# Two-block transformer on one core: first down projection of the second feed-forward accumulates onto a residual that ScalarE puts into PSUM

## Chip, cores and metric

The kernel runs on one core of one Trainium2 chip. The metric is the device time of one execution in microseconds. Before the change the median of three runs is 1496.56 us (1496.21 to 1496.62).

## What is computed

Two transformer blocks over 512 tokens of width 1024, in f32. The first has a mixed attention stage and a gated feed-forward; the second has two kinds of attention, a cross-attention, and at its end the feed-forward that matters here:

```python
def second_block(x, ...):
        ...
        h = rms_norm(x, norm_mlp[l])
        x = x + jnp.square(jax.nn.relu(h @ w_up[l])) @ w_down[l]
    return rms_norm(x, norm_final)
```

`w_up` is 1024 x 4096 and `w_down` 4096 x 1024.

## The kernel before

All activations lie transposed, features on the partitions: `x` is 8 chunks of 128 features x 512 tokens. Every f32 operand of a large product is split into a high part and a rest (`wh`, `wl` for weights, `hh`, `hl` or `ah2`, `al2` for activations), and a product is three matmuls of 128x128 by 128x512 (`three`, L1166 to L1170). Weights come as a stream of panels, 512 KB each, which hold 8 tiles of 128x128; a panel is 24 matmuls. The ring has four slots: SyncE loads a panel into `stage`, ScalarE copies it to `wh` (`hi`, L521 to L528), VectorE writes the rest `wl` (`lo`, L754 to L764). `hi` of a panel waits until TensorE is done with the panel four earlier, since it overwrites its `wh`.

The order on each engine is written out by hand, with semaphores between them. The second feed-forward runs as two halves of 2048 hidden features, A and B:

- Up: four rounds of four panels (`up_body`, one for each engine). TensorE makes a unit of 128 hidden features in one of PSUM's banks 0 to 3. VectorE scales it out of PSUM into `tmp` (L769), makes the rest of the weight panel four ahead (L764), squares it behind a relu (L2111), ScalarE copies the high part into `ah2` (L516), VectorE makes the rest `al2` (L2102).
- Down: eight chunks of 128 output features, each of two panels, so 48 matmuls over the 16 hidden units (`down_loop`). The first matmul of a chunk overwrites its bank, the others accumulate. At the end of a chunk VectorE adds the bank to `x` (L2125) and counts `evac`. ScalarE has nothing to do there but the weight copies.

TensorE goes from the last up panel of half A straight on to the first down panel. Of each chunk of the down projection `begin` (L1172 to L1176) waits for the panel's `wl` and for the eviction of the bank's last user, four units before:

```python
    def begin(p, e):
        pe.wait_ge(s.lo_ready, p.index + 1)
        if e is not None:
            pe.wait_ge(s.evac, e - 3)
```

ScalarE's last round of half A is `up_body(P_UP_A, FH // 4 - 1, False, 0)`, followed by `down_loop(P_DOWN_A, E_DOWN_A, False)`. In it, `hi` at `u == 3` prepares the fourth down panel and waits for the last up panel to be done. Half B has the same shape; its down projection (`last` is true) is tied to the final norm and is not changed.

Of the kernel before, what the change touches and what calls it, by code (L numbers as in the profile page):

```python
# [25 lines left out]
ALU = mybir.AluOpType  # L26
ACT = mybir.ActivationFunctionType
AX_X = mybir.AxisListType.X
# [3 lines left out]
KT = D // P  # L32
T = 512
# [25 lines left out]
FH = FF2 // P // 2  # L59
# [83 lines left out]
def semaphores(nc):  # L143

    s = Names()

    def named(names):
        return [nc.alloc_semaphore(name) for name in names.split()]
# [10 lines left out]
        "sums col_done mean_ready pow_done")  # L159
    (s.rs_ready, s.row_done, s.row_ready, s.u_ready) = named(  # L160
        "rs_ready row_done row_ready u_ready")
    (s.va_gelu, s.ln_mean, s.ln_pow, s.v_normed) = named(
        "va_gelu ln_mean ln_pow v_normed")
    (s.ws_masked, s.spatial_done, s.pooled, s.poolmm_done) = named(
        "ws_masked spatial_done pooled poolmm_done")
    (s.lam_dots, s.lam_exps, s.v_done, s.qk_hi) = named(
        "lam_dots lam_exps v_done qk_hi")
    (s.qk_ready, s.v_hi, s.v_ready, s.bias_in) = named(
        "qk_ready v_hi v_ready bias_in")
    (s.score_done, s.scored, s.negated, s.exped) = named(  # L170
# [338 lines left out]
def scalar_program(nc, act, s, b, dram, scratch, line_dram, out):  # L509
    A = nc.scalar.activation  # L510
# [75 lines left out]
    act.wait_ge(s.line_copied, 1)  # L586
    act.dma_start(line_dram, b.lines[0:HEADS, :]).then_inc(s.lines_out, 16)
    hi(Panel(P_POOL + 1 + RING))
    act.wait_ge(s.lam_dots, 1)
    A(b.lam_e, b.lam_d, ACT.Exp).then_inc(s.lam_exps, 1)  # L590

    act.wait_ge(s.lines_out, 16)
# [122 lines left out]
    for i in range(2):  # L715
        for c in range(4):
            k = 4 * i + c
# [29 lines left out]
def vector_program(nc, dve, s, b):  # L747
    V = nc.vector
# [66 lines left out]
    lam = b.early[:, 768:1024].rearrange("p (a c d) -> p a c d", a=2, c=2)  # L815
    prod = b.tmp[:, 0, 0:128].rearrange("p (a d) -> p a d", a=2)
    st.link(V.tensor_tensor(prod, lam[:, :, 0, :], lam[:, :, 1, :], ALU.mult))
    V.tensor_reduce(b.lam_d, prod, AX_X, ALU.add).then_inc(s.lam_dots, 1)
    dve.wait_ge(s.consts_in, 16)


# [10 lines left out]
    for t in range(TT):  # L832
        ins = V.tensor_scalar(b.va[:, t, :], b.ps[:, 2 + t // 2, 256 * (t % 2):256 * (t % 2) + 256],
                              b.rs[:, t:t + 1], None, ALU.mult)
# [8 lines left out]
        st.link(V.bn_stats(b.ln_stats[:, 6 * t:6 * t + 6], b.va[:, t, :]))  # L843
        st.link(V.bn_aggr(b.ln_mv[:, 2 * t:2 * t + 2], b.ln_stats[:, 6 * t:6 * t + 6]))
    var = b.ln_mv.rearrange("p (t c) -> p t c", c=2)
    V.tensor_scalar(b.ln_var, var[:, :, 1], 1e-5, None, ALU.add).then_inc(s.ln_mean, 1)
    evac_row(Panel(P_POOL + 1), E_POOL + 1, b.xb[:, 1, 16:], 1)
    lo(Panel(P_POOL + 1 + RING))
    dve.wait_ge(s.ln_pow, 1)
# [36 lines left out]
    with dve.Fori(0, 2) as i:  # L886
        for u in range(RING):
            e = E_Q + u
# [121 lines left out]
    for i in range(2):  # L1010
        for u in range(4):
            j = 4 * i + u
            p = Panel(P_PROJ + u + RING * i)
# [104 lines left out]
def gpsimd_program(nc, pool, s, b):  # L1118
    G = nc.gpsimd
    G.memset(b.lines[0:HEADS, T:LINE], NEG).then_inc(s.lines_set, 1)  # L1120

    pool.wait_ge(s.early_in, 64)
    G.affine_select(out=b.ws[:], in_=b.ws[:], compare_op=ALU.is_ge, fill=0.0, base=0,
                    pattern=[[0, 4], [1, P]], channel_multiplier=-1).then_inc(s.ws_masked, 1)

    def power(n):
        pool.wait_ge(s.mean_ready, n)
        G.tensor_tensor(b.rs, b.mean, b.expo[:, 0:4], ALU.pow).then_inc(s.pow_done, 1)

    power(1)  # L1130
    pool.wait_ge(s.ln_mean, 1)
    G.tensor_tensor(b.ln_rs, b.ln_var, b.expo[:, 0:4], ALU.pow).then_inc(s.ln_pow, 1)
    pool.wait_ge(s.omean_ready, 1)
    G.tensor_tensor(b.ors, b.omean, b.expo, ALU.pow).then_inc(s.opow_done, 1)
    power(2)

    pool.wait_ge(s.mean_ready, 3)
    G.tensor_tensor(b.rsa, b.mean, b.expo[:, 0:4], ALU.pow).then_inc(s.pow_a, 1)
    pool.wait_ge(s.mean_b, 1)
    G.tensor_tensor(b.rs, b.mean, b.expo[:, 0:4], ALU.pow).then_inc(s.pow_done, 1)  # L1140
    pool.wait_ge(s.mmean_ready, 1)
    G.tensor_tensor(b.mrs, b.mmean, b.expo[:, 0:MT], ALU.pow).then_inc(s.mpow_done, 1)
    pool.wait_ge(s.pv_done, 12)
    pool.wait_ge(s.v_ready, 8)
    pool.wait_ge(s.turned_ready, 48)
    G.memset(b.a[:], 0.0).then_inc(s.a_cleared, 1)
    pool.wait_ge(s.panel_done, P_VG + 4)
    G.memset(b.ke[:], 0.0).then_inc(s.ke_cleared, 1)

    for n in range(2):  # L1150
        pool.wait_ge(s.gmean_ready, n + 1)
        G.tensor_tensor(b.grs[:, 8 * n:8 * n + 8], b.gmean[:, 8 * n:8 * n + 8], b.expo[:, 0:8],
                        ALU.pow).then_inc(s.gpow_done, 1)
    for n in (4, 5):
        power(n)
    for half in range(2):
        pool.wait_ge(s.mean_ready, 6 + half)
        pair = slice(2 * half, 2 * half + 2)
        G.tensor_tensor(b.rs[:, pair], b.mean[:, pair], b.expo[:, 0:2], ALU.pow).then_inc(s.pow_done, 1)
# [3 lines left out]
def tensor_program(nc, pe, s, b):  # L1163
    MM = nc.tensor.matmul

    def three(out, wh, wl, xh, xl, start, stop):  # L1166

        MM(out, wh, xh, start=start, stop=False, skip_group_check=True)  # L1168
        MM(out, wh, xl, start=False, stop=False, skip_group_check=True)  # L1169
        return MM(out, wl, xh, start=False, stop=stop, skip_group_check=True)  # L1170
# [8 lines left out]
        wh, wl = parts_of(b, p)  # L1179
        return wh[:, a:a + n], wl[:, a:a + n]  # L1180

    def features(p, e, slot, xh=None, xl=None, tiles=range(KT), last=KT, width=T, ready=None, between=None):


        xh, xl = (b.hh, b.hl) if xh is None else (xh, xl)
        begin(p, e)
        for n, k in enumerate(tiles):
            for step in (between or {}).get(n, ()):
                step()
            if ready:  # L1190
                ready(k)
            wh, wl = w(p, P * n)
            ins = three(b.ps[:, slot, 0:width], wh, wl, xh[:, k, 0:width], xl[:, k, 0:width], k == 0, k == last - 1)
        ins.then_inc(s.panel_done, 1)

    def column_sums(n, sums):
# [269 lines left out]
def block2_scalar(nc, act, s, b, dram, scratch, A, AR, hi, row, x_parts, x_square, residual_loop, exp_pair):  # L1466
# [207 lines left out]
    residual_loop(P_XO, E_XO, "norm_mlp", 4)  # L1674


    def up_body(p0, i, first, base):
        for u in range(4):
            hi(Panel(p0 + u + RING, RING, i))
            if first and u == 0:  # L1680
                row(5)
            act.wait_ge(s.acted2, base + 4 * i + u + 1)
            AR(b.ah2[:, 4 * i + u, :], b.tmp[:, u % 2, :], ACT.Copy).then_inc(s.act2_hi, 1)

    def down_loop(p0, e0, last):
        if last:
            act.wait_ge(s.sums, 46)
        def body(i):
            for c in range(4):
                k = 4 * i + c  # L1690
                for m in range(2):
                    hi(Panel(p0 + 2 * c + m + RING, 8, i))
                if last and k == KT - 1:
                    act.wait_ge(s.sums, 45 + k)
                    for half in range(2):
                        act.wait_ge(s.evac, e0 + k + 1 + half)
                        tok = slice(M * half, M * half + M)
                        A(b.tmp[:, 1, tok], b.x[:, k, tok], ACT.Square).then_inc(s.x_squared, 1)
                elif last:
                    act.wait_ge(s.sums, 45 + k)  # L1700
                    act.wait_ge(s.evac, e0 + k + 1)
                    x_square(k, c % 2)
                    AR(b.x[:, k, :], b.x[:, k, :], ACT.Copy, scale=col(b, "norm_final", k)).then_inc(s.x_second, 1)

        body(0)
        body(1)

    up_body(P_UP_A, 0, True, 0)
    with act.Fori(1, FH // 4 - 1) as i:
        up_body(P_UP_A, i, False, 0)  # L1710
    up_body(P_UP_A, FH // 4 - 1, False, 0)
    down_loop(P_DOWN_A, E_DOWN_A, False)
    with act.Fori(0, FH // 4 - 1) as i:
        up_body(P_UP_B, i, False, FH)
# [5 lines left out]
def block2_vector(nc, dve, s, b, st, lo, evac_row, mean, x_rest, x_sum, residual_loop, score_pair):  # L1720
# [394 lines left out]
    def down_loop(p0, e0, last):  # L2115
        def body(i):
            for c in range(4):
                k = 4 * i + c
                if last and k == KT - 1:
                    continue  # L2120
                for m in range(2):
                    p = Panel(p0 + 2 * c + m, 8, i)
                    dve.wait_ge(s.panel_done, p.index + 1)
                    if m == 1:
                        V.tensor_tensor(b.x[:, k, :], b.x[:, k, :], b.ps[:, (e0 + c) % 4, :],  # L2125
                                        ALU.add).then_inc(s.evac, 1)
                    lo(p.plus(RING))
                if last:
                    x_sum(c % 2, 40 + k + 1, 46 + k)

        body(0)
        body(1)
# [53 lines left out]
def block2_tensor(nc, pe, s, b, MM, three, begin, w, features, column_sums, row, spread, x_ready, tokens, score, turn,  # L2186
# [289 lines left out]
    def up_body(p0, e0, i, first):  # L2476
        for u in range(4):
            features(Panel(p0 + u, RING, i), e0 + u + RING * i, (e0 + u) % 4,
                     ready=x_ready(32) if first and u == 0 else None,
                     between={1: [lambda: row(5)]} if first and u == 2 else None)  # L2480
            if first and u == 0:
                column_sums(5, 45)

    def down_loop(p0, e0, base):
        with pe.Fori(0, 2) as i:
            for c in range(4):
                for m in range(2):
                    features(Panel(p0 + 2 * c + m, 8, i), e0 + c + 4 * i if m == 0 else None, (e0 + c) % 4,
                             xh=b.ah2, xl=b.al2, tiles=range(KT * m, KT * m + KT), last=FH,
                             ready=(lambda k: pe.wait_ge(s.act2_ready, base + k + 1)) if c == 0 else None)  # L2490

    up_body(P_UP_A, E_UP_A, 0, True)
# [163 lines left out]
```

## Time and profile before

| | |
|---|---|
| median of three runs | 1496.56 us |
| span of the profiled execution | 1494.7 us |
| TensorE busy | 1485.1 us (99%) |
| VectorE busy | 876.2 us (59%) |
| ScalarE busy | 565.4 us (38%) |
| mean granted TensorE clock | 0.999 |

The profiled execution is one of the program's executions under the profiler; its span goes from its first to its last instruction, and no separate device time is recorded for it. The median of the runs is 1.9 us above that span. Half A's down projection runs from 1223.3 to 1310.3 us. Matmuls are pipelined: one row of the timeline lasts 0.39 us, but the next starts 0.23 us after it. In a timeline the first column is the start, the second the duration, and what stands in brackets is how long the engine sat idle before the row and what ended that. A row for `PEld` is a weight load, beside the matmuls.

### The profile page before, as it was taken

What the parts mean: (1) busy time and instruction counts of PE and PEld (TensorE: products, weight loads), DVE (VectorE), ACT (ScalarE), POOL (GpSimd) and SP (SyncE); (2) the same over time, 40 slices, a digit from 0 to 9 for tenths busy, and PEclk for the clock granted to TensorE, in tenths of its full rate; (3) what the DMA queues carried; (4) which work ended last, traced back from release to release, by engine and by line L of the source; (5) the groups of instructions that cost most, each with busy time, mean ns of one, the idle gap of its engine ahead of it and who ended that gap; (6) DMA issues with size and microseconds to landing.
All of it is one profiled execution on the core that took longest, in us unless ns stands there. A gap on an engine that the chain in (4) does not pass through costs nothing.

```text
span 1494.7 us, 20331 instructions
## 1 busy us (share of the span) xinstructions
PE 1485.1 (99%) x7240; PEld 1226.2 (82%) x7240; DVE 876.2 (59%) x1425; ACT 565.4 (38%) x836; POOL 24.2 (2%) x21
## 2 busy tenths in 40 slices
PE   9999999999999999999999999999999999999998
PEld 7878888888888888888888887888888888888887
DVE  6737764775665655443468877965665653255433
ACT  5215553333433333323325656444443331123231
POOL 0000000000000000000000000000000000000000
PEclk9999999999999999999999999999999999999999
DMA  6623222223322232333333223322122322333221
GB/s 234 226 87 97 77 91 85 85 83 101 112 88 95 98 98 98 99 102 110 113 99 106 94 97 102 110 76 84 61 81 85 109 91 96 98 99 98 99 71 57
DMA packets 44445, 149.17 MB, mean 100 GB/s; under 512 B 4792, under 2 KB 7352, under 8 KB 44260
## 3 DMA queue, kind: packets, MB, share of 16 engines
q1 hardware_dynamic: 39840, 138.43, 28.3%
q10 hardware_dynamic: 4548, 9.96, 1.9%
q8 instruction: 39, 0.64, 0.2%
q14 instruction: 18, 0.15, 0.0%
HBM read 146.24 MB, written 6.06 MB: 102 GB/s over the span
## 4 chain that ended last, share of the span: by engine, by line
PE 98%; issue 0%; DMA 0%; DVE 0%; ACT 0%; SPq 0%; POOLq 0%; POOL 0%; DVEq 0%; ACTq 0%
PE ps L1168 31%; PE ps L1170 31%; PE ps L1169 31%; PE ps L1319 1%; PE ps L1332 1%; PE ps L2340 1%; PE ps L1209 0%; DMA x<-x_dram 0%; PE ps L1202 0%; PE ps L2360 0%; PE ps L1377 0%; PE ps L2372 0%; PE ps L2440 0%; PE ps L2285 0%; PE ps L1274 0%
## 5 line engine op out<-in xcount | busy, mean ns | idle before, releaser
L528 ACT ACTIVATE wh<-stage 128x1024 fp32r<-128x1024 f32 x254 | 268.9, 1059 | 544.3 <-PE ps L1170 540.0
L1168 PE MATMUL ps<-hh,wh 128*128 128x512 f32 x1088 | 430.7, 396 | 0.3 <-DVE wl L764 0.3
L1170 PE MATMUL ps<-hh,wl 128*128 128x512 f32 x1088 | 424.3, 390 | 0.0
L1169 PE MATMUL ps<-hl,wh 128*128 128x512 f32 x1088 | 423.6, 389 | 0.0
L764 DVE TENSOR_TENSOR wl<-stage,wh 128x1024 fp32r<-128x1024 f32 x253 | 309.3, 1223 | 185.2 <-ACT wh L528 184.7
L1168 PEld LDWEIGHTS ps<-hh,wh 128*128 128x128 f32 x1088 | 204.3, 188 | 46.7 <-issue 3.9
L1170 PEld LDWEIGHTS ps<-hh,wl 128*128 128x128 f32 x1088 | 204.2, 188 | 43.5
L1169 PEld LDWEIGHTS ps<-hl,wh 128*128 128x128 f32 x1088 | 204.5, 188 | 39.8
L1168 PE MATMUL ps<-ah,wh 128*128 128x512 f32 (+1 forms) x448 | 171.7, 383 | 0.0
L1170 PE MATMUL ps<-ah,wl 128*128 128x512 f32 (+1 forms) x448 | 171.5, 383 | 0.0
L1169 PE MATMUL ps<-al,wh 128*128 128x512 f32 (+1 forms) x448 | 171.5, 383 | 0.0
L769 DVE TENSOR_TENSOR tmp<-ps,rrow 128x512 f32<-128x512 f32 x86 | 59.3, 690 | 98.2 <-PE ps L1170 87.0
L1170 PEld LDWEIGHTS ps<-ah,wl 128*128 128x128 f32 x448 | 84.3, 188 | 16.9
L1169 PEld LDWEIGHTS ps<-al,wh 128*128 128x128 f32 x448 | 84.3, 188 | 16.9
L1168 PEld LDWEIGHTS ps<-ah,wh 128*128 128x128 f32 x448 | 84.3, 188 | 16.8
L516 ACT ACTIVATE ah<-tmp 128x512 f32 (+1 forms) x54 | 34.1, 632 | 108.1 <-DVE tmp L2111 64.5
L1168 PE MATMUL ps<-wh,hh 128*128 128x512 f32 (+1 forms) x128 | 46.8, 366 | 0.0
L1170 PE MATMUL ps<-wh,hl 128*128 128x512 f32 (+1 forms) x128 | 46.4, 363 | 0.0
L1169 PE MATMUL ps<-wl,hh 128*128 128x512 f32 (+1 forms) x128 | 46.4, 362 | 0.0
L615 ACT ACTIVATE s<-s,neg 128x128 f32<-128x128 f32 (+3 forms) x64 | 35.5, 555 | 19.6 <-DVE neg L935 19.6
L2125 DVE TENSOR_TENSOR x<-x,ps 128x512 f32<-128x512 f32 x15 | 10.3, 688 | 49.6 <-PE ps L1170 49.6
L769 DVE TENSOR_TENSOR gb<-ps,rrow 128x512 f32<-128x512 f32 x22 | 15.2, 692 | 40.5 <-PE ps L1170 33.1
(340 smaller groups left out, 1839.3 us busy)
## 6 DMA issues: line engine op xcount, KB each, us to landing
stage<-stream_dram SPq DMA_DIRECT2D x254, 512.0 KB, 3.3
bias_lines<-bias_line ACTq DMA_DIRECT2D x1, 3840.0 KB
bias<-bias_lines ACTq DMA_DIRECT2D x4, 512.0 KB, 4.8
x<-x_dram SPq DMA_DIRECT2D x3, 512.0 KB, 7.3
out_dram<-x SPq DMA_DIRECT2D x12, 128.0 KB, 1.9
bias<-bias_lines ACTq DMA_DIRECT2D x4, 256.0 KB, 2.9
mem<-mem_dram ACTq DMA_DIRECT2D x1, 1024.0 KB, 4.8
stage<-stream_dram SPq DMA_DIRECT2D x2, 256.0 KB, 4.0
```

The source lines that it names most:

```text
L516: return A(*args, **kw)
L528: A(parts_of(b, p)[0], b.stage[:, p.slot, :], ACT.Copy).then_inc(s.hi_ready, 1)
L615: A(sc, sc, ACT.Exp, bias=b.neg[:, n:n + 1], accum_out=b.sums[:, n:n + 1]).then_inc(s.exped, 1)
L764: V.tensor_tensor(wl, b.stage[:, p.slot, :], f32(wh), ALU.subtract).then_inc(s.lo_ready, 1)
L769: V.tensor_tensor(dst, b.ps[:, slot, :], b.rrow[:], ALU.mult).then_inc(s.evac, 1)
L1168: MM(out, wh, xh, start=start, stop=False, skip_group_check=True)
L1169: MM(out, wh, xl, start=False, stop=False, skip_group_check=True)
L1170: return MM(out, wl, xh, start=False, stop=stop, skip_group_check=True)
L1319: ins = MM(b.ps[:, 4 + 2 * (qb % 2) + c, 0:width], q[part, tok], k[part, 0:width], start=n == 0, stop=n == 2, skip_group_check=True)
L1332: ins = nc.tensor.transpose(b.ps[:, 5 + kb % 2, P * (qb - kb):P * (qb - kb) + P], b.s[:, c, at:at + P], b.ident)
L2125: V.tensor_tensor(b.x[:, k, :], b.x[:, k, :], b.ps[:, (e0 + c) % 4, :], ALU.add).then_inc(s.evac, 1)
L2340: ins = MM(b.ps[:, (6 if level % 2 else 4) + a, 64 * c:64 * c + 64], b.ke[part, level % 2, P * c:P * c + P], b.qe[part, level % 2, c, :], ...
```

## The change

In half A's down projection ScalarE copies chunk k of `x` into the chunk's PSUM bank before its products ("seed"), all 48 matmuls of the chunk accumulate, and VectorE copies the finished sum from PSUM to `x`. TensorE waits at each chunk for the semaphore `seeded` where it waited for `evac`; the wait for `evac` goes to the seed on ScalarE. Seeds 0 and 1 stand in the last up round, behind the weight copy at `u == 3`; seed k+2 stands behind the two weight copies of chunk k. The semaphores `lam_dots` and `ln_mean`, used once each near the start, become one, `dots_mean`, that counts to 2.

```diff
-    def features(p, e, slot, xh=None, xl=None, tiles=range(KT), last=KT, width=T, ready=None, between=None):
+    def features(p, e, slot, xh=None, xl=None, tiles=range(KT), last=KT, width=T, ready=None, between=None, opens=0):
...
-            ins = three(b.ps[:, slot, 0:width], wh, wl, xh[:, k, 0:width], xl[:, k, 0:width], k == 0, k == last - 1)
+            ins = three(b.ps[:, slot, 0:width], wh, wl, xh[:, k, 0:width], xl[:, k, 0:width], k == opens, k == last - 1)
...
-    def up_body(p0, i, first, base):
+    def up_body(p0, i, first, base, seeds=()):
         for u in range(4):
             hi(Panel(p0 + u + RING, RING, i))
+            if u == 3:
+                for k in seeds:
+                    seed(k)
...
+    def seed(k):
+
+        act.wait_ge(s.evac, E_DOWN_A + k - 3)
+        A(b.ps[:, (E_DOWN_A + k) % 4, :], b.x[:, k, :], ACT.Copy).then_inc(s.seeded, 1)
...
                 for m in range(2):
                     hi(Panel(p0 + 2 * c + m + RING, 8, i))
+                if not last and k + 2 < KT:
+                    seed(k + 2)
...
-    up_body(P_UP_A, FH // 4 - 1, False, 0)
+    up_body(P_UP_A, FH // 4 - 1, False, 0, (0, 1))
...
-                    if m == 1:
+                    if m == 1 and last:
                         V.tensor_tensor(b.x[:, k, :], b.x[:, k, :], b.ps[:, (e0 + c) % 4, :],
                                         ALU.add).then_inc(s.evac, 1)
+                    elif m == 1:
+                        V.tensor_copy(b.x[:, k, :], b.ps[:, (e0 + c) % 4, :]).then_inc(s.evac, 1)
...
-                    features(Panel(p0 + 2 * c + m, 8, i), e0 + c + 4 * i if m == 0 else None, (e0 + c) % 4,
-                             xh=b.ah2, xl=b.al2, tiles=range(KT * m, KT * m + KT), last=FH,
+                    if m == 0:
+                        pe.wait_ge(s.seeded, 4 * i + c + 1)
+                    features(Panel(p0 + 2 * c + m, 8, i), None, (e0 + c) % 4,
+                             xh=b.ah2, xl=b.al2, tiles=range(KT * m, KT * m + KT), last=FH, opens=-1,
```

How ScalarE's instructions stand at the end of the last up round and in the first chunks of the down projection (`wh_158` is the weights' high part, `ah_156` the activations'; a row ends with the semaphores that it waits for). Before:

```order
L516 ACTIVATE ah_156<-tmp 128x512 [waits vec_in,acted2]
L528 ACTIVATE wh_158<-stage 128x1024 [waits panel_done,load2]
L516 ACTIVATE ah_156<-tmp 128x512 [waits vec_in,acted2]
L528 ACTIVATE wh_158<-stage 128x1024 [waits panel_done,load3]
L528 ACTIVATE wh_158<-stage 128x1024 [waits panel_done,load0]
L528 ACTIVATE wh_158<-stage 128x1024 [waits panel_done,load1]
L528 ACTIVATE wh_158<-stage 128x1024 [waits panel_done,load2]
```

And with the change (L1691 is the seed):

```order
L516 ACTIVATE ah_156<-tmp 128x512 [waits vec_in,acted2]
L528 ACTIVATE wh_158<-stage 128x1024 [waits panel_done,load2]
L1691 ACTIVATE ps<-x 128x512 [waits evac] x2
L516 ACTIVATE ah_156<-tmp 128x512 [waits vec_in,acted2]
L528 ACTIVATE wh_158<-stage 128x1024 [waits panel_done,load3]
L528 ACTIVATE wh_158<-stage 128x1024 [waits panel_done,load0]
L1691 ACTIVATE ps<-x 128x512 [waits evac]
L528 ACTIVATE wh_158<-stage 128x1024 [waits panel_done,load1]
L528 ACTIVATE wh_158<-stage 128x1024 [waits panel_done,load2]
```

Two seeds stand between the weight copy of the fourth down panel and the copy of the last activation; from there on one seed stands behind each pair of weight copies.

TensorE at the start of the down projection, before:

```order
L1170 MATMUL ps<-hh,wl 128x512
L2493 REGISTER_ALU
L2493 COMPARE_AND_BRANCH
L2485 UNCONDITIONAL_BRANCH
L2485 ISA
L1176 ISA [waits lo_ready]
L1168 MATMUL ps<-ah_156,wh_158 128x512 [waits act2_ready,evac]
```

And with the change:

```order
L1170 MATMUL ps<-hh,wl 128x512
L2507 REGISTER_ALU
L2507 COMPARE_AND_BRANCH
L2497 UNCONDITIONAL_BRANCH
L2497 ISA
L1174 ISA [waits seeded]
L1168 MATMUL ps<-ah_156,wh_158 128x512 [waits act2_ready,lo_ready]
```

The instructions are the same in number; `seeded` stands where a wait stood before, and `evac` is gone from TensorE's side.

## Rows read from the trace of the kernel before

**Rows 1.** The page: span, and busy time of TensorE with its share
```profile
span 1494.7 us, 20331 instructions
...
PE 1485.1 (99%) x7240; PEld 1226.2 (82%) x7240; DVE 876.2 (59%) x1425; ACT 565.4 (38%) x836; POOL 24.2 (2%) x21
```

**Rows 2.** The page: the chain that ended last, shares by engine
```profile
PE 98%; issue 0%; DMA 0%; DVE 0%; ACT 0%; SPq 0%; POOLq 0%; POOL 0%; DVEq 0%; ACTq 0%
```

**Rows 3.** What TensorE waited for: total us, times, longest us
```profile
PE ps L1225 <- DVE rrow L790: 1.6, 1, 1.6
PE ps L2520 <- POOL small L1159: 1.0, 1, 1.0
PE ps L2513 <- ACT tmp L1698: 0.6, 1, 0.6
```

**Rows 4.** Timeline of ScalarE around the end of half A's up projection
```profile
1221.05 0.63 ACT L516 ACTIVATE ah<-tmp 128x512 fp32r<-128x512 f32 x1 [1.89 <-DVE tmp L2111]
1223.55 1.06 ACT L528 ACTIVATE wh<-stage 128x1024 fp32r<-128x1024 f32 x1 [1.86 <-PE ps L1170]
1226.50 0.63 ACT L516 ACTIVATE ah<-tmp 128x512 fp32r<-128x512 f32 x1 [1.89 <-DVE tmp L2111]
...
1234.43 1.06 ACT L528 ACTIVATE wh<-stage 128x1024 fp32r<-128x1024 f32 x1 [4.38 <-PE ps L1170]
```

**Rows 5.** Timeline of VectorE over the same stretch
```profile
1218.04 0.69 DVE L769 TENSOR_TENSOR tmp<-ps,rrow 128x512 f32<-128x512 f32 x1 [1.06 <-PE ps L1170]
...
1225.79 0.68 DVE L2111 SCALAR_TENSOR_TENSOR tmp<-tmp 128x512 f32<-128x512 f32 x1
...
1234.37 0.69 DVE L2125 TENSOR_TENSOR x<-x,ps 128x512 f32<-128x512 f32 x1 [2.99 <-PE ps L1170]
```

**Rows 6.** Timeline of TensorE: last up product, first down product, next up projection
```profile
1223.06 0.40 PE L1170 MATMUL ps<-hh,wl 128*128 128x512 f32 x1
...
1223.29 0.39 PE L1168 MATMUL ps<-ah,wh 128*128 128x512 f32 x1
...
1310.34 0.39 PE L1168 MATMUL ps<-hh,wh 128*128 128x512 f32 x1
```

**Rows 7.** Timeline of ScalarE at the start: operations queued behind a weight copy
```profile
15.94 1.06 ACT L528 ACTIVATE wh<-stage 128x1024 fp32r<-128x1024 f32 x1 [1.34 <-DMA stage<-stream_dram]
16.90 1.14 ACT L516 ACTIVATE tmp<-x 128x512 f32<-128x512 f32 x2
```

**Rows 8.** ScalarE operations that read PSUM: ns min/median/max
```profile
L1642 ACT ACTIVATE xth<-ps x8: 593/596/602, 1044.7 to 1097.8; 128x512 fp32r<-128x512 f32 x8
...
L1575 ACT ACTIVATE vg<-ps,small x4: 687/689/692, 919.1 to 923.1; 128x512 f32<-128x512 f32 x4
```

**Rows 9.** Timeline of all engines where TensorE waits in mid-stream
```profile
1097.96 1.29 DVE L2057 TENSOR_TENSOR xtl<-ps,xth 128x512 fp32r<-128x512 f32 x2 [2.58 <-ACT xth L1642]
...
1099.31 0.49 PE L1168 MATMUL ps<-xth,vxh 128*128 128x512 f32 x1 [0.24 <-DVE xtl L2057]
...
1099.64 0.39 PE L1169 MATMUL ps<-xtl,vxh 128*128 128x512 f32 x1
...
1100.99 0.60 ACT L1647 ACTIVATE oxh<-ps 128x512 fp32r<-128x512 f32 x1 [2.57 <-PE ps L1170]
1101.03 0.39 PE L1169 MATMUL ps<-xtl,vxh 128*128 128x512 f32 x1
...
1101.26 0.40 PE L1170 MATMUL ps<-xth,vxl 128*128 128x512 f32 x1
```

**Rows 10.** VectorE's plain copies out of PSUM: ns min/median/max
```profile
L1804 DVE COPY oa<-ps x8: 672/684/695, 810.2 to 894.9; 64x512 f32 x6, 64x512 f32<-64x512 f32 x2
```

**Rows 11.** Windows: us, busy (x) of PE PEld DVE ACT POOL, PEclk, DMA share, GB/s
```profile
1490.00:1491.00 1.00, 0.00 (x0) 0.00 (x0) 1.00 (x4) 0.00 (x0) 0.00 (x0) 0.95 0.80 262
1491.00:1492.00 1.00, 0.00 (x0) 0.00 (x0) 1.00 (x4) 0.00 (x0) 0.00 (x0) 0.50 1.02 342
...
0.00:1488.00 1488.00, 1484.67 (x7238) 1226.02 (x7238) 872.60 (x1415) 565.38 (x836) 23.54 (x20) 1.00 0.30 99
```

More of the change, by code:

```diff
@@ L161, in semaphores @@
         "rs_ready row_done row_ready u_ready")
-    (s.va_gelu, s.ln_mean, s.ln_pow, s.v_normed) = named(
-        "va_gelu ln_mean ln_pow v_normed")
+    (s.va_gelu, s.dots_mean, s.ln_pow, s.v_normed) = named(
+        "va_gelu dots_mean ln_pow v_normed")
     (s.ws_masked, s.spatial_done, s.pooled, s.poolmm_done) = named(
         "ws_masked spatial_done pooled poolmm_done")
-    (s.lam_dots, s.lam_exps, s.v_done, s.qk_hi) = named(
-        "lam_dots lam_exps v_done qk_hi")
+    (s.lam_exps, s.v_done, s.qk_hi, s.seeded) = named(
+        "lam_exps v_done qk_hi seeded")
     (s.qk_ready, s.v_hi, s.v_ready, s.bias_in) = named(
@@ L588, in scalar_program @@
     hi(Panel(P_POOL + 1 + RING))
-    act.wait_ge(s.lam_dots, 1)
+    act.wait_ge(s.dots_mean, 1)
     A(b.lam_e, b.lam_d, ACT.Exp).then_inc(s.lam_exps, 1)
@@ L817, in vector_program @@
     st.link(V.tensor_tensor(prod, lam[:, :, 0, :], lam[:, :, 1, :], ALU.mult))
-    V.tensor_reduce(b.lam_d, prod, AX_X, ALU.add).then_inc(s.lam_dots, 1)
+    V.tensor_reduce(b.lam_d, prod, AX_X, ALU.add).then_inc(s.dots_mean, 1)
     dve.wait_ge(s.consts_in, 16)
@@ L845, in vector_program @@
     var = b.ln_mv.rearrange("p (t c) -> p t c", c=2)
-    V.tensor_scalar(b.ln_var, var[:, :, 1], 1e-5, None, ALU.add).then_inc(s.ln_mean, 1)
+    V.tensor_scalar(b.ln_var, var[:, :, 1], 1e-5, None, ALU.add).then_inc(s.dots_mean, 1)
     evac_row(Panel(P_POOL + 1), E_POOL + 1, b.xb[:, 1, 16:], 1)
@@ L1130, in gpsimd_program @@
     power(1)
-    pool.wait_ge(s.ln_mean, 1)
+    pool.wait_ge(s.dots_mean, 2)
     G.tensor_tensor(b.ln_rs, b.ln_var, b.expo[:, 0:4], ALU.pow).then_inc(s.ln_pow, 1)
```

## Prediction

> **What bounds the kernel now.** I read the page's busy shares first: TensorE is busy for 1485.1 us of a span of 1494.7 us [rows 1]. The chain that ended last says the same from the other side: 98% of it is TensorE's own work [rows 2]. The list of what TensorE waited for is short, and its longest entry is 1.6 us, at the very start of the program; the next ones, 1.0 and 0.6 us, are in the tail behind the last projection [rows 3]. Between those two ends TensorE runs as a stream. So a change in the middle can gain nothing by relieving VectorE or ScalarE. It can only cost something, by making TensorE stand where it does not stand today, and what it stands is added to the time in full, since no later wait in the middle is there to swallow it.
>
> Then I read the three timelines around the place of the change, the end of the last up panel and the start of the first down panel. On TensorE the last up product starts at 1223.06 us and the first down product at 1223.29, the next slot of the stream [rows 6]. From there to 1310.34 us, where the next up projection begins [rows 6], lie 16 panels of 24 matmuls, so one slot is (1310.34 - 1223.29)/384 = 0.227 us. On ScalarE the weight copy for the panel four ahead (L528) starts at 1223.55 us [rows 4]. Its wait ends with the last up product, since it overwrites that panel's slot of the ring; then it takes 1.06 us. After it ScalarE sits idle for 1.89 us until VectorE has squared the last activation (the operation at 1225.79, 0.68 us long, [rows 5]), and copies that at 1226.50 [rows 4].
>
> **The change, part by part.**
>
> *The first seed.* This is the one term. In the new order seeds 0 and 1 stand on ScalarE right behind the weight copy at 1223.55, and TensorE's first down product waits for seed 0. Today that product waits for nothing that is late. Step by step, with today's clock times:
> - The weight copy starts at 1223.55 us, as today [rows 4]: nothing ahead of it changes.
> - A ScalarE operation queued behind such a copy starts 0.96 us after it, seen at the start of the program, where the copy begins at 15.94 and the next operation at 16.90 [rows 7]. So the seed starts at 1224.51. Its wait for the bank is long over: that bank was emptied by the first unit of the last up round, ahead even of the eviction at 1218.04 [rows 5].
> - No row of this trace has ScalarE writing to PSUM. The nearest rows of 128x512: copy from SBUF to SBUF 0.63 us [rows 4], copy from PSUM to SBUF 0.60 us, and a scaled one from PSUM 0.69 us [rows 8]. From below I take 0.51 us, what one of two queued copies adds: the pair of [rows 7] lasts 1.14 us where one lasts 0.63 us. I take 0.62, between the two plain copies, which are the nearest in kind; ends 0.51 and 0.69. The seed ends at 1225.13.
> - TensorE starts again 0.06 us after such a release: VectorE's pair ends at 1097.96 + 1.29 = 1099.25, the matmul that waited starts at 1099.31 [rows 9]. Here that is 1225.19.
> - A restart costs a little more than the gap: from the first matmul to the second it is 0.33 us in place of a slot (1099.31 to 1099.64), and the seven after that take 1.62 us against 7 x 0.227 = 1.59 [rows 9]. Together 0.13 us.
>
> The stall is 1225.19 - 1223.29 + 0.13 = 2.03 us. With the two ends of the seed it is 1.92 to 2.10, and I widen the upper end to 2.3 because this wait stands in the sequencer ahead of the matmul's other waits, which the row of [rows 9] does not have in the same form.
>
> The Trainium skill (ScalarE: Activation LUTs, under Step-by-step: what each stage is for) says that ScalarE writes faster to PSUM than to SBUF. By that rule the seed would lie at the 0.60 of the plain copy from PSUM or a little under, and the sum would be about 2.0 us in place of 2.03; no row here shows such a write.
>
> *The second seed and the last activation.* Seed 1 follows 0.51 to 0.63 us behind seed 0 and ends by 1225.8. The squared activation is there at 1226.47 (1225.79 + 0.68, [rows 5]), so both seeds fit in ScalarE's 1.89 us of idle time and the copy at 1226.50 is not moved, nor is what VectorE does after it. Nothing. Had they not fitted, the sixteenth activation is wanted by the sixteenth step of the first chunk only, 15 x 3 slots or 10.2 us on.
>
> *Seeds 2 to 7.* Each stands behind the two weight copies that chunk k releases, and is wanted when chunk k+2 starts. Seed 2 comes behind the copy at 1234.43 [rows 4], so at about 1235.4 to 1236.0; chunk 2 starts two chunks, 96 slots or 21.8 us, after 1223.29, at 1245.1. The cover is 9 us on every chunk, and PSUM banks are not short either: seed 4 wants the bank of chunk 0, emptied at 1234.37 [rows 5], more than 20 us before. ScalarE has 4.38 us idle ahead of each weight copy there [rows 4], so 0.62 us per 10.9 us delays no later copy. Nothing, unless the writes disturb the matmuls (a rival, below).
>
> *VectorE.* Eight additions of 0.69 us [rows 5] become eight copies out of PSUM. The nearest row, a copy of 64x512, takes 0.68 us [rows 10], so even the engine gains next to nothing, and what it gains is hidden: it waits for TensorE ahead of the eviction.
>
> *TensorE.* The wait for the eviction goes and the wait for the seed takes its place, one for one; the first product of each chunk adds onto the bank where it used to overwrite. Both are a slot of the same stream. Merging two old semaphores into one moves no instruction: the one that counts first is always the same. Nothing for both.
>
> **The sum**: +2.03 us, taken from the profiled execution, whose span is 1494.7 us [rows 1]: 1496.7. The median of the runs is 1496.56, 1.9 us above that span (what lies around the span), and the stall is in the span, so the time is 1496.56 + 2.03 = **1498.6 us**, 0.14% more. A measurement of this kernel tells about 0.2%, or 3.0 us, from no change; the forecast is a loss, but one that counts as the same.
>
> **The rivals.**
>
> *The clock falls in the stall* (ends slower). TensorE has stood nowhere in the middle for 2 us. What the trace has is the tail. From the start to 1488 us the mean granted clock is 1.00, the wait of 1.6 us [rows 3] among it; then, with the stream over, it is 0.95 on the mean of 1490 to 1491, a stretch in which TensorE does nothing at all, and 0.50, the 1.2 GHz level, from 1491 on [rows 11]. So no wait of up to 1.6 us brought it down, and that speaks against a fall after 2 us, though not by much. For it: nothing in the trace excludes it. Price: the only low stretch seen goes on from 1491 to the end at 1494.7, 3.7 us; a stream at half rate for as long loses 1.85 us on top, 3.9 us in all, 1500.4 us. It decides from the stall on in which the clock goes down to 0.50. The Trainium skill (TensorE: Matmul & The Clock Gate, the section on why this matters for your kernels) warns that idle gaps of TensorE in mid-kernel bring back the low clock; by it this stall is the place to look.
>
> *PSUM writes by ScalarE hold the matmuls up.* Six seeds run beside products. If TensorE stood for all of each, that is 6 x 0.62 = 3.7 us more, 1502.3 us. Against it: while ScalarE reads PSUM at 1100.99, the matmuls at 1101.03 and 1101.26 keep a slot of 0.23 [rows 9]. For it: a read is not a write.
>
> *TensorE does not wait* (0 us, 1496.6 us): if the seed could be issued ahead of the weight copy, or the time from the last up product to the seed were hidden. Against it stand the order of ScalarE's instructions and the 1.86 us that it waits for TensorE's last up product [rows 4]. Faster than before has no mechanism that I can find: no wait on TensorE is shortened.
>
> **How the numbers follow.** Forecast 0.85; no wait 0.04; clock 0.06; held up 0.02; 0.03 for what I have not seen. The range goes from 1498.1 (a stall of 1.9 less 0.4 of scatter between runs, about the spread of the three shown) to 1499.4 (2.3 and 0.5); it leaves out the rivals, and a little of the forecast. Slower by over 0.2% is the clock, the holding up and a part of the unknown: 0.10. Faster 0.01, same 0.89.
>
> **What would show it.** In the new trace TensorE should show one wait for ScalarE's seed on the first line of the product, about 1.7 us by the profile's reckoning (a matmul's modelled end, 1223.06 + 0.40 = 1223.46, lies behind its slot, so 1225.19 - 1223.46), and no wait at the other seven seeds. ScalarE should show the copy at 1223.55, the first seed at 1224.5 and the second 0.5 us later; VectorE's copy some 0.7 us. From there on everything should stand 2.0 us later than today, the tail too, with the clock at 1.00 through it. A clock under 1.00 behind the stall, a wait at a second seed, a slot longer than 0.227 us beside a seed, or the first down product at 1223.3 would each prove one step wrong.

## The result, and the profile after

The changed kernel takes 1500.06 us (median of 15 runs, 1498.74 to 1500.79) against 1496.42 us before (15 runs, 1496.12 to 1496.95): 3.6 us, or 0.24%, more by the medians. The ratio on record, which isn't that of the medians, is 1.0021, with a 95% interval of 1.0014 to 1.0029. The prediction was 1498.6 us, with a range to 1499.4.

The 15 runs are not one cloud. Six lie between 1498.74 and 1499.32 us and nine between 1500.05 and 1500.79, with nothing between; the kernel before shows no such gap. The lower group is where the forecast put the whole. The profiled execution, at 1499.32 us, is of the lower group.

| | before | after |
|---|---|---|
| median | 1496.42 us | 1500.06 us |
| span of the profiled execution | 1494.7 us | 1497.6 us |
| TensorE busy | 1485.1 us | 1485.9 us |
| ScalarE busy | 565.4 us | 569.2 us |
| VectorE busy | 876.2 us | 875.8 us |

What TensorE waited for, after (total us, times, longest us):

```profile
PE ps L1168 <- ACT ps L1691: 1.9, 1, 1.9
PE ps L1225 <- DVE rrow L790: 1.6, 1, 1.6
PE ps L2534 <- POOL small L1159: 1.0, 1, 1.0
PE ps L1168 <- DVE hl L775: 0.7, 1, 0.7
PE ps L2527 <- ACT tmp L1708: 0.6, 1, 0.6
```

The seed stands at the top, with a single wait; the second, third and fifth rows answer to [rows 3]. The fourth, 0.7 us, lies at the start of the program, where `x` arrives, and is why everything in this profile is about half a microsecond later than before even ahead of the change.

ScalarE's timeline after, the place of [rows 4]:

```profile
1224.06 1.06 ACT L528 ACTIVATE wh<-stage 128x1024 fp32r<-128x1024 f32 x1 [1.85 <-PE ps L1170]
1225.02 1.10 ACT L1691 ACTIVATE ps<-x 128x512 f32<-128x512 f32 x2
1227.01 0.63 ACT L516 ACTIVATE ah<-tmp 128x512 fp32r<-128x512 f32 x1 [0.88 <-DVE tmp L2121]
1231.67 1.06 ACT L528 ACTIVATE wh<-stage 128x1024 fp32r<-128x1024 f32 x1 [4.03 <-PE ps L1170]
1237.11 1.06 ACT L528 ACTIVATE wh<-stage 128x1024 fp32r<-128x1024 f32 x1 [4.38 <-PE ps L1170]
1238.08 0.58 ACT L1691 ACTIVATE ps<-x 128x512 f32<-128x512 f32 x1
```

And TensorE's, the place of [rows 6], with the first product of the next up projection as its last row:

```profile
1223.58 0.39 PE L1170 MATMUL ps<-hh,wl 128*128 128x512 f32 x1
1225.85 0.47 PE L1168 MATMUL ps<-ah,wh 128*128 128x512 f32 x1 [1.89 <-ACT ps L1691]
1226.16 0.39 PE L1169 MATMUL ps<-al,wh 128*128 128x512 f32 x1
...
1238.44 0.39 PE L1169 MATMUL ps<-al,wh 128*128 128x512 f32 x1
1238.67 0.39 PE L1170 MATMUL ps<-ah,wl 128*128 128x512 f32 x1
...
1313.02 0.39 PE L1168 MATMUL ps<-hh,wh 128*128 128x512 f32 x1
```

The two seeds follow the weight copy 0.96 us after its start and fit ahead of the copy of the last activation, as worked out. TensorE's next slot would have been 1223.58 + 0.227 = 1223.81, and it starts at 1225.85: 2.04 us. From there to the next up projection it takes 87.17 us, where the kernel before took 87.05: 0.12 us for the restart. The stall costs 2.16 us. Beside the third seed (1238.08 to 1238.66) the slots keep their 0.23 us, and no other seed is waited for.

So this profile has a stall of 2.2 us, most of the 2.6 us by which the lower group's median (1498.98) lies above the kernel before, and nothing of the 1.2 us between the medians of the two groups on this chip.

### The profile page after: what moved, and what is told of

Its sections match the earlier page's. It is cut to its first block, busy times and chain, and to the rows that moved or that the text cites. A ratio compares the mean times of both kernels' runs of the same rounds, so it can differ in the third digit from the quotient of the medians.

```text
span 1497.6 us, 20339 instructions
## 1 busy us (share of the span) xinstructions
PE 1485.9 (99%) x7240; PEld 1226.2 (82%) x7240; DVE 875.8 (58%) x1425; ACT 569.2 (38%) x844; POOL 23.5 (2%) x21
## 4 chain that ended last, share of the span: by engine, by line
PE 98%; issue 0%; DMA 0%; DVE 0%; ACT 0%; SPq 0%; POOLq 0%; POOL 0%; DVEq 0%; ACTq 0%
PE ps L1168 31%; PE ps L1170 31%; PE ps L1169 31%; PE ps L1319 1%; PE ps L1332 1%; PE ps L2352 1%; PE ps L1209 0%; DMA x<-x_dram 0%; PE ps L1202 0%; PE ps L2372 0%; PE ps L1377 0%; PE ps L2384 0%; PE ps L2452 0%; PE ps L2297 0%; PE ps L1274 0%
## 5 line engine op out<-in xcount | busy, mean ns | idle before, releaser
L2112 DVE TENSOR_TENSOR al<-tmp,ah 128x512 f32 (+1 forms) x32 | 22.2, 692 | 27.4 <-ACT ah L516 27.4
```

Of the source, the lines that this page charges most:

```text
L2112: V.tensor_tensor(b.al2[:, j, :], b.tmp[:, half, :], f32(b.ah2[:, j, :]), ALU.subtract).then_inc(s.act2_ready, 1)
```

## The experiments

### Again, earlier, elsewhere, longer

Four kernels on one chip, where the kernel before took 1496.30 us (median of 30 runs). The first is the changed kernel unaltered.

> The changed kernel again, unaltered. Its 15 runs lay in two groups, 5 from 1498.7 to 1499.3 us and 10 from 1500.05 to 1500.8, mean granted clock 0.998 and 0.997 to 0.998. Theory A (the stall of 2.2 us at the first seed and nothing else; the groups are something of the machine that every kernel could show): one group near +2.2 us. Theory B (the stall, and in some executions TensorE's granted clock goes down behind it for a few us): the two groups again, about 1.1 us apart, and in a profile of the slower group a window under 1.00 right behind 1225 us. Theory C (ScalarE's PSUM writes hold products up in some executions): the two groups, with slots over 0.227 us beside seeds and the clock at 1.00.

(The groups of the first 15 runs are 6 and 9, not 5 and 10.)

Measured: 1498.99 us, 11 runs, ratio 1.0021 (1.0012 to 1.003). Six runs lie from 1498.05 to 1498.99, five from 1499.79 to 1500.50. The mean granted clock is 0.998 or 0.999 in the first six, 0.997 in four of the other five. Theory A falls, since the groups come back on another chip and the kernel before has none. The profile was again one of the lower group, with the clock at 1.00 on the mean of 1223 to 1240 us, so B against C stayed open in this run. The mean clock of a whole execution is a weak sign by itself: it was 0.998 in the profiled execution of the changed kernel, whose clock stayed up behind the stall, since it also counts the low clock of the tail, where TensorE has little or nothing left to do.

The second moves the first two seeds ahead of the weight copy:

```diff
         for u in range(4):
-            hi(Panel(p0 + u + RING, RING, i))
             if u == 3:
                 for k in seeds:
                     seed(k)
+            hi(Panel(p0 + u + RING, RING, i))
```

> Seeds 0 and 1 go ahead of the weight copy of the same unit, where ScalarE has 1.9 us of idle time; all else as in the change. Theories A and B: no stall, so no fall of the clock either; the time is that of the kernel before within 0.3 us, in one group. Theory C: no stall, but the groups stay, up to 1.1 us over the kernel before.

Measured: 1496.34 us, 11 runs from 1495.65 to 1496.71, ratio 0.9999 (0.999 to 1.0008). One group, no loss. ScalarE's timeline of it:

```profile
1221.24 0.63 ACT L516 ACTIVATE ah<-tmp 128x512 fp32r<-128x512 f32 x1 [1.89 <-DVE tmp L2121]
1221.78 1.10 ACT L1691 ACTIVATE ps<-x 128x512 f32<-128x512 f32 x2
1223.73 1.06 ACT L528 ACTIVATE wh<-stage 128x1024 fp32r<-128x1024 f32 x1 [0.85 <-PE ps L1170]
```

The seeds are now in the idle time of the unit before, and the weight copy starts when it always did, at TensorE's release. All eight seeds still write to PSUM and all products still accumulate onto them, so those are free, in this trace and in the time: Theory C falls with this run.

The third keeps the order and the wait, but nothing goes to PSUM:

```diff
-        A(b.ps[:, (E_DOWN_A + k) % 4, :], b.x[:, k, :], ACT.Copy).then_inc(s.seeded, 1)
+        A(b.diag[:, k % 2, :], b.x[:, k, :], ACT.Copy).then_inc(s.seeded, 1)
```

(with the product's own start and VectorE's addition as before the change)

> The seeds stand where the change puts them and TensorE waits for them, but they write to an unused buffer in SBUF; the first product overwrites the bank and VectorE adds, as before the change. The seed is then 0.63 us in place of 0.58, the stall 0.05 us longer. Theories A and B: the same as the changed kernel, +2.2 us (A) or +2.2 and +3.4 us in two groups (B). Theory C: +2.2 us alone, one group, with nothing written to PSUM.

Measured: 1499.96 us, 11 runs from 1497.93 to 1501.83, ratio 1.0022 (1.0013 to 1.0031). Four runs lie at 1499.12 or below, seven at 1499.82 or above. The whole loss is there, with its two groups, without a byte written to PSUM. And this time the profiled execution, 1500.67 us, was one of the upper group. Its windows (us, then busy time and count of PE, PEld, DVE, ACT, POOL, then the granted clock, DMA share, GB/s):

```profile
1225.00:1226.00 1.00, 0.49 (x2) 0.47 (x3) 1.00 (x2) 0.69 (x2) 0.00 (x0) 1.00 0.00 0
1226.00:1227.00 1.00, 1.00 (x4) 0.82 (x4) 0.51 (x1) 0.46 (x1) 0.00 (x0) 0.66 0.00 0
1227.00:1229.00 2.00, 2.00 (x6) 1.54 (x6) 0.69 (x1) 0.17 (x1) 0.00 (x0) 0.50 0.77 262
1229.00:1230.00 1.00, 1.00 (x5) 0.77 (x4) 0.00 (x0) 0.00 (x0) 0.00 (x0) 0.63 0.00 0
1230.00:1240.00 10.00, 10.00 (x46) 8.26 (x45) 2.45 (x3) 2.64 (x3) 0.00 (x0) 1.00 0.14 52
```

The first down product started at 1225.51. The clock is still full then, goes to 0.50 within the next microsecond and is back before 1230. TensorE reads as busy all through; it is the count of products that gives it away: 6 have a part in the two microseconds from 1227, where the first profile of the changed kernel has 11. This is Theory B.

The fourth makes the stall longer, by a wait for both seeds:

```diff
     def down_loop(p0, e0, base):
+        pe.wait_ge(s.seeded, 2)
         with pe.Fori(0, 2) as i:
```

> The changed kernel, but the first down product waits for both seeds, so the stall is longer by one queued copy, 0.5 us. Theory A: +2.7 us, one group. Theory B: +2.7 us or more, and the fall of the clock in more of the executions than the 10 of 15 of the changed kernel, or for longer: most runs at +3.9 us or over. Theory C: the groups of the changed kernel moved by 0.5 us, as often as there.

Measured: 1500.60 us, 8 runs, ratio 1.0026 (1.0015 to 1.0036). Three runs lie from 1499.04 to 1499.66, five from 1500.58 to 1501.07: +2.7 to +3.4 us and +4.3 to +4.8. In its profile, of the upper group, the clock is down before the first product has started (1225.91):

```profile
1225.00:1226.00 1.00, 0.09 (x1) 0.12 (x1) 1.00 (x2) 0.47 (x1) 0.00 (x0) 0.85 0.00 0
1226.00:1229.00 3.00, 3.00 (x7) 2.36 (x8) 1.01 (x2) 0.63 (x1) 0.00 (x0) 0.50 0.54 175
1229.00:1230.00 1.00, 1.00 (x6) 0.79 (x5) 0.00 (x0) 0.00 (x0) 0.00 (x0) 0.95 0.00 0
```

The wait of this profile is 2.60 us, 0.7 more than the changed kernel's, where every theory had 0.5; two of the three lower runs lie at +3.4 us. That the clock falls more often, five of eight, can't be told from the changed kernel's share with so few runs.

### Shorter stalls, a filled one, and the changed kernel caught

Four kernels on another chip, where the kernel before took 1496.64 us (median of 31 runs). Two start from the early seeds and put a shorter wait into the same place:

```diff
     def down_loop(p0, e0, base):
+        pe.wait_ge(s.hi_ready, P_DOWN_A + 4)
         with pe.Fori(0, 2) as i:
```

> Both seeds stand early, as in the run without a stall, but the first down product now waits for ScalarE's weight copy that starts at the end of the last up panel: a stall of about 1.6 us with restart, 0.6 us shorter than the changed kernel's. Stall alone: +1.6 us, one group. Stall and clock: +1.6 us, and in fewer executions than the changed kernel's about half a fall of the clock that adds 0.7 to 1.7 us; if a stall this short never brings it down, one group.

Measured: 1498.37 us, 11 runs from 1497.51 to 1499.09, ratio 1.0011 (1.0002 to 1.002), +1.7 us. The runs spread over 1.6 us without a gap like the changed kernel's, about as wide as the kernel before (1.5 us). That is one group at the wait's own price; a single fall among the eleven would not stand out, and is not excluded.

```diff
     def down_loop(p0, e0, base):
+        pe.wait_ge(s.evac, E_DOWN_A)
         with pe.Fori(0, 2) as i:
```

> The same with a wait for VectorE's eviction of the last up unit, which ends about 0.7 us after that unit: a stall of 1.1 to 1.3 us with restart. Stall alone: +1.2 us, one group. Stall and clock: +1.2 us, and the clock down in few executions or none.

Measured: 1497.86 us, 11 runs from 1497.11 to 1498.43, ratio 1.0008 (0.9999 to 1.0017), +1.2 us by the medians, and no run set apart. The waits that these two profiles show, one row each:

```profile
PE ps L1168 <- ACT wh L528: 1.6, 1, 1.6
```
```profile
PE ps L1168 <- DVE tmp L769: 1.2, 1, 1.2
```

The next is the decisive one. The changed kernel waits just as long, but TensorE works through the wait, on products into an unused bank that nobody reads:

```diff
     def down_loop(p0, e0, base):
+        for n in range(9):
+            MM(b.ps[:, 5, :], b.ah2[:, 0, 0:P], b.ah2[:, 0, :], start=True, stop=True, skip_group_check=True)
         with pe.Fori(0, 2) as i:
```

> The changed kernel, with nine extra products of 128x512 into an unused bank in front of the wait for the first seed: 9 x 0.227 = 2.0 us of work that nobody reads, so TensorE is busy through the stall. Theory of the clock: the first real product starts when the seed is there, as in the changed kernel, +2.1 us, but the clock stays at 1.00 and all executions lie in one group near 1498.4. If the groups come from anything else about the wait or the seeds, they stay.

Measured: 1498.62 us, 11 runs from 1498.30 to 1498.95, ratio 1.0015 (1.0006 to 1.0024), +2.0 us. One narrow group, at the lower of the changed kernel's two. TensorE's timeline:

```profile
1223.02 0.40 PE L1170 MATMUL ps<-hh,wl 128*128 128x512 f32 x1
1223.25 2.21 PE L2498 MATMUL ps<-ah 128*128 128x512 f32 x9
1225.31 0.47 PE L1168 MATMUL ps<-ah,wh 128*128 128x512 f32 x1
```

And the window around it:

```profile
1223.00:1240.00 17.00, 17.00 (x76) 13.90 (x75) 6.36 (x7) 5.31 (x7) 0.00 (x0) 1.00 0.20 66
```

The real product starts 2.29 us after the last up product, where the changed kernel's starts 2.27 after it. (The nine products alone would set the same start, 10 slots or 2.27 us on, so they just fill the wait.) The delay is the same, and it is TensorE's idleness, not the delay, that brings the second group.

And the changed kernel itself, unaltered, once more:

> The changed kernel once more, for the share of its executions in which the clock falls and for a profile of one: about half of the runs near 1500.3, the others near 1498.7. If the profile is one of the slower ones, it shows windows at 0.50 for 2 to 3.4 us right behind the stall and slots of 0.43 us in them; at 1.00 throughout if it is one of the others.

Measured: 1500.06 us, 9 runs, ratio 1.0022 (1.0012 to 1.0032): three from 1498.64 to 1499.29, six from 1500.01 to 1501.21. This time the profile, at 1500.06 us, caught it. Its windows behind the stall:

```profile
1225.00:1225.50 0.50, 0.48 (x2) 0.46 (x3) 0.50 (x2) 0.29 (x1) 0.00 (x0) 0.96 0.00 0
1225.50:1226.00 0.50, 0.50 (x2) 0.35 (x2) 0.50 (x2) 0.00 (x0) 0.00 (x0) 0.50 0.00 0
1226.00:1228.50 2.50, 2.50 (x7) 1.97 (x6) 0.84 (x2) 0.63 (x1) 0.00 (x0) 0.50 0.68 197
1228.50:1229.00 0.50, 0.50 (x3) 0.36 (x3) 0.00 (x0) 0.00 (x0) 0.00 (x0) 0.63 0.17 66
1229.00:1240.00 11.00, 11.00 (x50) 9.11 (x49) 2.96 (x3) 2.61 (x3) 0.00 (x0) 1.00 0.14 48
```

And its products in that stretch:

```profile
1222.74 0.39 PE L1170 MATMUL ps<-hh,wl 128*128 128x512 f32 x1
1225.02 0.47 PE L1168 MATMUL ps<-ah,wh 128*128 128x512 f32 x1 [1.89 <-ACT ps L1691]
...
1226.47 0.63 PE L1169 MATMUL ps<-al,wh 128*128 128x512 f32 x1
1226.90 0.63 PE L1170 MATMUL ps<-ah,wl 128*128 128x512 f32 x1
...
1228.61 0.52 PE L1168 MATMUL ps<-ah,wh 128*128 128x512 f32 x1
1228.97 0.39 PE L1169 MATMUL ps<-al,wh 128*128 128x512 f32 x1
```

The wait is the 1.89 us of the first profile. From 1225.02 to 1228.97 lie ten slots; at full clock, with the same restart, they take 0.31 + 9 x 0.23 = 2.38 us, here 3.95. The fall costs 1.57 us. By the windows the clock is low for 0.04 + 0.5 + 2.5 + 0.37 = 3.4 us. A slot at the 1.2 GHz level is 0.43 us, not quite two of 0.227.

### The idea where the addition is on the path

In the tail VectorE's addition does stand between the last product and the norm. The last kernel keeps the early seeds and also seeds the last chunk of half B, in its two halves; ScalarE squares straight from PSUM and VectorE copies to `x` behind it:

```diff
-                        act.wait_ge(s.evac, e0 + k + 1 + half)
+                        act.wait_ge(s.panel_done, P_END - 1 + half)
...
-                        A(b.tmp[:, 1, tok], b.x[:, k, tok], ACT.Square).then_inc(s.x_squared, 1)
+                        A(b.tmp[:, 1, tok], b.ps[:, (e0 + k + half) % 4, tok], ACT.Square).then_inc(s.x_squared, 1)
...
+                    if k == 5:
+                        for half in range(2):
+                            tok = slice(M * half, M * half + M)
+                            A(b.ps[:, (e0 + KT - 1 + half) % 4, tok], b.x[:, KT - 1, tok], ACT.Copy).then_inc(s.seeded, 1)
...
-        dve.wait_ge(s.panel_done, P_END - 1 + half)
-        V.tensor_tensor(b.x[:, k7, tok], b.x[:, k7, tok], b.ps[:, (E_DOWN_B + k7 + half) % 4, tok],
-                        ALU.add).then_inc(s.evac, 1)
+        dve.wait_ge(s.x_squared, 48 + half)
+        V.tensor_copy(b.x[:, k7, tok], b.ps[:, (E_DOWN_B + k7 + half) % 4, tok]).then_inc(s.evac, 1)
...
+    pe.wait_ge(s.seeded, KT + 2)
...
-            ins = three(b.ps[:, e % 4, tok], wh, wl, b.ah2[:, k, tok], b.al2[:, k, tok], k == 0, k == FH - 1)
+            ins = three(b.ps[:, e % 4, tok], wh, wl, b.ah2[:, k, tok], b.al2[:, k, tok], False, k == FH - 1)
```

> Seeds 0 and 1 early, and the idea put where VectorE's addition does lie on the path: the last chunk of half B. ScalarE seeds its two halves of 256 tokens after chunk 5, all its products accumulate, ScalarE squares the sum straight from PSUM, and VectorE copies it to x afterwards, beside the column sums. In the tail the addition of 256 columns (about 0.45 us) and one handover go from the chain last product, addition, square, column sums: -0.4 to -0.5 us against the kernel before if the rest of the tail keeps up, 0 if VectorE or the output transfers set the end anyway. Either way it lies within 0.2% of the kernel before; the tail's timeline decides.

Measured: 1496.42 us, 11 runs, against 1496.48 for the kernel before on that chip; ratio 1.0 (0.9991 to 1.0009). The tail of its profile, all engines, from the last product on:

```profile
1485.83 0.28 PE L1170 MATMUL ps<-ah,wl 128*128 128x256 f32 x1
...
1486.57 0.42 DVE L2168 COPY x<-ps 128x256 f32<-128x256 f32 x1 [0.81 <-ACT tmp L1708]
1486.59 0.61 PE L2530 MATMUL ps<-consts,tmp 128*128 128x1 f32 x4
1486.91 0.74 DVE L2182 TENSOR_TENSOR x<-x,ps 128x256 f32<-128x256 f32 x2
1487.57 0.15 DVE L2173 TENSOR_SCALAR small<-ps 128x2 f32<-128x2 f32 x1
...
1488.55 0.69 PE L2537 MATMUL ps<-consts,small 128*128 128x128 f32 x2 [1.35 <-POOL small L1159]
1489.28 2.40 DVE L2182 TENSOR_TENSOR x<-x,ps 128x256 f32<-128x256 f32 x7 [0.84 <-PE ps L2537]
```

The same place in the trace of the kernel before:

```profile
1486.05 0.28 PE L1170 MATMUL ps<-ah,wl 128*128 128x256 f32 x1
...
1487.30 0.61 PE L2513 MATMUL ps<-consts,tmp 128*128 128x1 f32 x4 [0.62 <-ACT tmp L1698]
1487.94 0.16 DVE L2158 TENSOR_SCALAR small<-ps 128x2 f32<-128x2 f32 x1 [0.48 <-PE ps L2513]
...
1489.40 2.41 DVE L2167 TENSOR_TENSOR x<-x,ps 128x256 f32<-128x256 f32 x7 [0.57 <-PE ps L2520]
```

The column sums come 0.76 us behind the last product where it was 1.25, so the 0.49 us is won. Then VectorE, which now has the copy and two scalings in its queue, takes up the mean 0.98 us after the column sums began, where it was 0.64, and the two transposes take 0.69 us in place of the 0.43 before, behind a longer wait and with the clock down to 0.58 on the mean of 1488 to 1489. The final scaling starts 3.45 us behind the last product, against 3.35. In this profile what was won is given back before the end, and in the time no version here beats the kernel before.

Of that, VectorE's 0.34 us follow from the edit. The other part, the two slow transposes, can't be put down to it, since they are also seen in tails that nothing changed; this is the row in the first profile of the changed kernel, where they take 0.69 us too:

```profile
1491.61 0.69 PE L2534 MATMUL ps<-consts,small 128*128 128x128 f32 x2 [1.03 <-POOL small L1159]
```

There the clock is 0.85 on the mean of 1491.00 to 1491.60 us, so it fell within the wait of 1.03 us ahead of this row; in the profile with early seeds the same row takes 0.43 us behind the same wait. Another order on VectorE was not tried. By the 0.34 us it could return some 0.3 us, an estimate, which these timings can't tell from nothing.

## Why the prediction was wrong

**The bound** was read rightly. Nothing was gained anywhere, and the stall of one engine in the middle came through to the end in full.

**The stall** was sized at 2.03 us; the profile shows 2.16. Its steps: the seed starts 0.96 us behind the weight copy, as forecast. The seed lasts 0.58 us, not 0.62, and below the plain copy out of PSUM (0.60): the copy of the same shape into SBUF in the third experiment lasts 0.615 us, so the Trainium skill's rule (ScalarE: Activation LUTs, under Step-by-step: what each stage is for) that PSUM is the faster target agrees with these two numbers, by 0.03 us. TensorE starts 0.25 us after the seed's end (1225.60 to 1225.85), not 0.06: here the forecast was four times too low, and the widened upper end of 2.3 covered it. The two other profiles of the changed kernel show the same 0.25 us (1224.35 to 1224.60 and 1224.77 to 1225.02); behind the seed into SBUF it is 0.33. Which part of the handover takes it was not tested. The restart took 0.12 us, forecast 0.13.

**The terms costed at nothing** were nothing: the second seed, seeds 2 to 7, VectorE's copies (0.69 us each, as the additions), the accumulation in place of an overwrite. The run with early seeds has all of them, and takes 0.9999 (0.999 to 1.0008) of the time before.

**What failed is the chance given to the clock.** The rival "the clock falls in the stall" was given 6 in 100, on the argument that no wait of up to 1.6 us had brought it down. Over the 35 runs of the changed kernel on record, 20 lie at 1499.79 us or above and 15 at 1499.32 or below, so it happens in more than half. (A run is put into a group by its time; the clock itself was seen in three of the 35, low in the one profiled in the upper group and full in the two of the lower.) Both halves of the mechanism were on paper, and the price nearly right: 1.85 us on top was the estimate, 1.57 us is what the profile shows, and 1.4 us lie between the medians of the two groups (1500.26 and 1498.84; 1.2 to 1.8 us taken chip by chip). The estimate was high because it took the low stretch at 3.7 us, up to the end of the trace, where the profiles show 3.4. Where it went wrong was in reading waits of up to 1.6 us as evidence on one of 2 us. The experiments show how much lies between them. With a wait of 1.2 or 1.6 us no second group shows in 11 runs each; with 1.9 us the upper group has 20 of 35, with 2.0 us (the seeds into SBUF) seven of 11, and with 2.6 us five of eight. What decides it in the single execution, with the same kernel and the same wait, stays open.

The trace of the kernel before supported the 6 in 100 even less than the prediction says. Its wait of 1.6 us lies from 0 to 1.56 us, ahead of TensorE's first product, so it is no wait behind a stream. And the rows of the tail hold a fall that was read past. This is TensorE's last row:

```profile
1488.93 0.43 PE L2520 MATMUL ps<-consts,small 128*128 128x128 f32 x2 [1.03 <-POOL small L1159]
```

TensorE stands from 1489.36 us on, and a mean clock of 0.95 for 1490 to 1491 [rows 11] means that it went from 1.00 to 0.50 at about 1490.9, some 1.5 us later. The changed kernel's tail above shows a fall within a wait of 1.03 us. TensorE has little to do in the tail ahead of that (it is busy for 0.58 us of 1490 to 1491 there), so these waits are not the same as one behind full work; but that no short standstill brings the clock down could not be read from this trace.

The Trainium skill's warning (TensorE: Matmul & The Clock Gate, the section on why this matters for your kernels) that idle gaps in mid-kernel bring back the low clock agrees with the three profiles at 0.50 and with the run whose gap was filled. The prediction cited it as the place to look, and then hardly weighed it.

A second fault is one of form. The forecast was a single time with a narrow range, for something that either happens or doesn't in each execution. With a rival of 1.9 us on top of the forecast, and a median that jumps to it as soon as it happens in half of the runs, a range that stopped at 1499.4 rested wholly on those 6 in 100.

## What to carry to other kernels

Here a new wait of TensorE, the bounding engine, cost its length, 2.2 us, and in more than half of the executions about 1.5 us on top through its clock. The cure was to place the producer ahead of what else is released at the same moment: two copies moved ahead of a weight copy, and the loss is gone. To know whether a step is costly or only badly placed, run it once moved: the run with early seeds separates the two in one go. And before preferring an accumulation over an addition, look who waits for the addition: in the middle of this stream nobody did.

## What the runs showed of the hardware that was not expected

- The same kernel on the same chip takes two times, 1.2 to 1.8 us apart, by whether the granted clock goes to 0.50 behind the same wait of 1.89 us. In the two profiles of the upper group with that wait or nearly (1.89 and 2.02 us) it is low for 3.4 us, which begin after TensorE has taken up work again: some 0.5 us after in one (1225.02 to about 1225.5) and about 0.8 us after in the other. With the wait of 2.6 us it is down before the first product. In the tail it fell within a wait of 1.03 us, so the length of the last wait alone doesn't decide it.
- Busy time doesn't show it. In the window from 1226.00 to 1228.50 TensorE is busy for 2.50 of 2.50 us at half the rate; only the clock column and the slot of 0.43 us tell.
- Nine products that nobody reads make the changed kernel faster by 1.4 us in the median on that chip (1498.62 against 1500.06); in the profiled execution the clock stays at 1.00.
- ScalarE's write of 128x512 f32 to PSUM, 0.583 us, beside TensorE's products into another bank changes no slot.
